# Two barriers of a layer replaced by waits for single producers, in a decoder step of retention, gated linear attention and RWKV-7

## The reference

```python
h = rmsnorm(x, norm_mix)
proj = h @ w_in                      # columns for retention, GLA, RWKV-7 and three merge gates
y_ret, S_ret = retention_branch(...) # 8 heads, key 64, value 128
y_gla, S_gla = gla_branch(...)       # 4 heads, key 128, value 256
y_rw, S_rw, shift = rwkv7_branch(...)# delta rule, 16 heads of 64
merged = (sigmoid(g0) * (y_ret @ wb[0]) + sigmoid(g1) * (y_gla @ wb[1])
          + sigmoid(g2) * (y_rw @ wb[2]))
x = x + merged @ w_out
h = rmsnorm(x, norm_ffn)
x = x + (swiglu(h) if layer == 0 else top2_of_8_experts(h))
```

## Time and profile before

| | us |
|---|---|
| median of 3 runs (2856.09 to 2858.42) | 2857.78 |
| the profiled execution, its own time | 2859.5 |
| span of that execution in the trace | 2857.3 |
| TensorE (PE) busy | 2717.4 (95%) |
| VectorE (DVE) busy | 841.7 (29%) |
| ScalarE (ACT) busy | 571.9 (20%) |
| mean granted TensorE clock | 0.979 of full |

### The profile page before, as it was taken

One profiled execution on the slowest core, in us unless ns is written; L12 is line 12 of the kernel. 1 busy time (PEld: TensorE's weight loads), 2 busy tenths in 40 slices (PEclk: granted clock), 3 DMA queues, 4 the chain that ended last, 5 costly groups with the idle time before them and its releaser, 6 DMA issues. The chain is left out here.

```text
span 2857.3 us, 78627 instructions
## 1 busy us (share of the span) xinstructions
PE 2717.4 (95%) x34890; PEld 2218.9 (78%) x34890; DVE 841.7 (29%) x2465; ACT 571.9 (20%) x1736; POOL 0.2 (0%) x4
## 2 busy tenths in 40 slices
PE   8999989999799999999998999989799999999998
PEld 5777877666577776777786676667799999999997
DVE  2023664555411001112465555531301111110111
ACT  2123332332200000113333323310110111111011
POOL 0000000000000000000000000000000000000000
PEclk9999999999999999999999999979799999999999
DMA  6333432222243444323343222224399999999985
GB/s 216 97 120 141 145 122 72 67 73 73 69 138 124 136 133 144 106 91 132 120 149 118 72 73 64 66 83 139 147 348 372 336 327 366 367 332 346 370 331 219
DMA packets 144460, 495.95 MB, mean 174 GB/s; under 512 B 18608, under 2 KB 23344, under 8 KB 141648
## 3 DMA queue, kind: packets, MB, share of 16 engines
q1 hardware_dynamic: 144208, 492.24, 48.6%
HBM read 471.88 MB, written 20.29 MB: 172 GB/s over the span
## 5 line engine op out<-in xcount | busy, mean ns | idle before, releaser
L378 PEld LDWEIGHTS psum<-work,ring 128*64 128x64 f32 x16896 | 699.9, 137 | 27.9 <-issue 14.5
L378 PE MATMUL psum<-work,ring 128*64 128x96 f32 x16896 | 714.9, 246 | 3.0 <-issue 1.7
L293 PE MATMUL psum<-hT,ring 128*128 128x288 f32 x2048 | 562.7, 416 | 0.0
L293 PEld LDWEIGHTS psum<-hT,ring 128*128 128x128 f32 x2048 | 375.6, 192 | 95.9 <-ACT work L389 2.7
L371 PE MATMUL psum<-hT,ring 128*128 128x288 f32 x1024 | 256.1, 411 | 7.8 <-PEq L188 7.8
L371 PEld LDWEIGHTS psum<-hT,ring 128*128 128x128 f32 x1024 | 196.8, 193 | 65.1 <-issue 10.2
L1400 ACT ACTIVATE work<-psum 128x256 f32<-128x256 f32 (+4 forms) x304 | 101.1, 370 | 426.3 <-PE psum L1314 100.1
L1803 PE MATMUL psum<-hT,ring 128*128 128x288 f32 x704 | 172.6, 409 | 1.7 <-DVE hT L1877 1.7
L1803 PEld LDWEIGHTS psum<-hT,ring 128*128 128x128 f32 x704 | 134.7, 191 | 39.6 <-issue 2.1
L2401 DVE TENSOR_TENSOR work<-psum,work 128x96 f32<-128x96 f32 x176 | 45.3, 257 | 380.8 <-PE psum L378 368.6
L2350 ACT ACTIVATE work<-psum 128x96 f32<-128x96 f32 x176 | 44.1, 250 | 410.0 <-PE psum L378 410.0
(11 more groups left out here) (399 smaller groups left out, 2892.9 us busy)
## 6 DMA issues: line engine op xcount, KB each, us to landing
ring<-w_ff_dram SPq DMA_DIRECT2D x540, 512.0 KB, 5.4
ring<-w_mix_dram SPq DMA_DIRECT2D x256, 512.0 KB, 3.7
ring<-w_ff_dram SPq DMA_DIRECT2D x72, 384.0 KB, 4.7
work<-s_gla_dram SPq DMA_DIRECT2D x8, 1024.0 KB, 4.8
gla_s_out<-work SPq DMA_DIRECT2D x8, 1024.0 KB, 4.6
work<-s_ret_dram SPq DMA_DIRECT2D x8, 512.0 KB, 4.7
ret_s_out<-work SPq DMA_DIRECT2D x8, 512.0 KB, 3.0
work<-s_rw_dram SPq DMA_DIRECT2D x16, 256.0 KB, 2.6
```

Of the source, the lines that this page charges most:

```text
L293: mm = nc.tensor.matmul(out, ring[:, s, k, :], rhs[:, k, :], start=(k == 0), stop=(k == KT - 1))
L378: mm = nc.tensor.matmul(out[64 * c:64 * c + 64], ring[:, s, k, 64 * c:64 * c + 64], rhs[:, k0 + k, :], start=(k0 + k == 0), stop=(k0 + k = ...
```

## The change

Each layer's projections and retention now share one block, and so do the delta rule and the merge. An engine runs from one program into the next with no barrier between. Two waits are added on TensorE: before retention for all 24 results of the projections to have left their banks, and in the second slab of the merge, before each of its eight products, for the tile of `y_rw` that it reads. The landing place of the 32-bit masks moves from column 8704 to 12000 of `work`. The semaphores of the two phases of a block are cleared together at the block's end.

```diff
-    masks32 = work[:, 8704:8704 + MASKS.shape[1]].bitcast(U32)
+    masks32 = work[:, 12000:12000 + MASKS.shape[1]].bitcast(U32)
...
-    def retention(nc, block, sig, layer):
+    def retention(nc, block, sig, layer, projected):
...
         @block.tensor
         def _(pe):
+            pe.wait_ge(projected("bank_free"), 3 * RING)
             with pe.Fori(0, PAIRS) as i:
...
-    def mix_out(nc, block, sig, layer):
+    def mix_out(nc, block, sig, layer, delta):
...
-                slab_products(pe, n % RING, bank[n % 4][:, 0:T], y_rw if n % 2 else [hT[:, k, :] for k in range(KT)])
+                x = y_rw if n % 2 else [hT[:, k, :] for k in range(KT)]
+                for k in range(KT):
+                    if n == 1:
+                        pe.wait_ge(delta("y"), k + 1)
+                    mm = nc.tensor.matmul(bank[n % 4][:, 0:T], ring[:, n % RING, k, :], x[k], start=(k == 0),
+                                          stop=(k == KT - 1))
+                mm.then_inc(slab_done, 1)
...
-        with phase(nc, f"in{layer}") as (block, sig):
-            project_in(nc, block, sig, layer)
-        with phase(nc, f"ret{layer}") as (block, sig):
-            retention(nc, block, sig, layer)
+        with phase(nc, f"in{layer}") as (block, projected):
+            project_in(nc, block, projected, layer)
+            retention(nc, block, Signals(nc, f"ret{layer}"), layer, projected)
         with phase(nc, f"gla{layer}") as (block, sig):
             gated_linear(nc, block, sig, layer)
-        with phase(nc, f"rw{layer}") as (block, sig):
-            rwkv(nc, block, sig, layer)
-        with phase(nc, f"mix{layer}") as (block, sig):
-            mix_out(nc, block, sig, layer)
+        with phase(nc, f"rw{layer}") as (block, delta):
+            rwkv(nc, block, delta, layer)
+            mix_out(nc, block, Signals(nc, f"mix{layer}"), layer, delta)
```

## The result

The changed kernel takes 2842.14 us, a median of 5 runs (2833.58 to 2846.41), against 2857.78 before (5 runs, 2856.09 to 2860.39). The ratio is 0.9942, with a 95% interval of 0.9923 to 0.9960: 11 to 22 us faster, 16.6 at the ratio itself. The ratio compares the means of the runs; the two medians lie 15.6 apart. Forecast were 2842.1 us and 0.9945.

A forecast was written before the change was run, and what follows sets the result against it. TensorE, busy 95% of the span, was taken as the bound, so time is won only where it idles or runs at the lower clock. 7.9 + 7.8 + 1.4 − 1.4 = 15.7 us off 2857.78 gave 2842.1, range 2835 to 2849.

The forecast's parts named there:

- Seam A: Projections to retention: without the barrier, 3.95 and 3.90 us gained in the two layers, together 7.9.
- the second wait: Before the first GLA slab: TensorE waits some 0.3 us for ScalarE's grant behind its table load.
- The drain behind a table load: Skill's rule, left out of the sum: grant before the first GLA slab 1.4 us later per layer, total gain 12.9.
- The clock at seam A: Projections to retention: 3.5 us of the 7.9 gained come from avoiding the lower clock.
- Seam B: Delta rule to merge: without the barrier, 7.8 us of idle time and 1.4 of clock gained.
- the clock's part of the gain: Merge's first slab: less time lost to the low clock, 1.4 us gained (0.6 to 2.2).
- The clears: End of each merged block: clearing two phases' semaphores together, with all engines waiting, loses 1.4 us.
- Only idle time is won: Rival: clock falls at projections to retention, returns no earlier at the merge; gain 10.8 us, 2847.0; chance 0.13.
- The barrier stays in another form: Rival: a block's two programs are still kept apart by something all engines pass; no change, 2857.8; chance 0.04.
- the code is not there: Rival: engines stall at the seams for the next program's instructions; slower, 2877.4 us; chance 0.03.
- The last step changes its clock: Rival: delta rule's last step, 6.0 us apart between layers, changes; 2848.1 or 2836.1 us; chance 0.12 each side.
- a later phase gives time back: Sign of being wrong: GLA and feed-forward should start earlier by the forecast sums and last as long as before.

The follow-up runs named there:

- filled barriers: Kernel before, barriers kept, with products nobody reads in TensorE's time in front of them at both seams; ratio 0.9990, 2.9 us faster.
- seam A alone: Changed kernel with delta rule and merge put back in separate blocks; ratio 0.9962 to the kernel before, 10.9 us faster.
- seam B alone: Changed kernel with projections and retention put back in separate blocks; ratio 0.9971 to the kernel before, 8.3 us faster.
- e4: Changed kernel, wait before retention cut to 22 of 24 results, VectorE granting the first GLA slabs; ratio 0.9941 to the kernel before.
- e5: e4 with the merge's first slab done in pieces within the delta rule's last step; ratio 0.9903 to the kernel before, median 2832.1 us.
- e6: e5 with seven of the eight products of the merge's second slab also moved into the last step; ratio 0.9910 to the kernel before.
- e7: Kernel before with 80 unused semaphores more in each of six phases; ratio 1.0016, 4.6 us slower.
- e8: e5 with three products of the merge's second slab done ahead of the variance; ratio 0.9885 to the kernel before, median 2827.8 us.
- e9: e5 with three products that nobody reads in the places where e8 moves products; ratio 0.9913 to the kernel before.

## Why the prediction was right

**Seam A** was put at 7.9 us and measured 7.8. Two things inside it were off and cancelled. TensorE starts its swaps 0.36 us after ScalarE's copy ends, where the sum had it start at once (0.44 behind the last slab): idle is 0.80, not 0.4 to 0.6. For that the second wait, for ScalarE's grant behind the table load, does not show at all, since the load (to 124.16) is over before the swaps are. The wait of some 0.3 us that the sum put there was not seen. The transposes start 5.74 us behind the last slab; 5.7 was forecast. The copies for the transposes did hide, and so did SP's load of the state. The drain behind a table load that the Trainium skill states ("ScalarE: Activation LUTs", What ACT_TABLE_LOAD costs) is not seen here either: the load starts at 1241.87 in layer 1 and ScalarE's next copy at 1243.16, 1.29 later, where the page's total would be 2.66.

**The clock at seam A**, 3.5 us of the 7.9, measured 3.4 (the ledger's 7.8 less 4.4 of idle). It is shown by the filled barriers: the same slab in 3.88 us with the barrier left in place.

**Seam B** was put at 9.2 and measured 9.0. The idle time went whole. The second slab starts 5.57 and 5.34 us behind the variance (4.9 to 5.7 forecast), the clock came back 4.3 and 4.1 us after the variance began (3.5 to 5.0). The slab lost 1.7 and 1.5 us to the low clock, at the upper end of the 1.05 to 1.85, so the clock's part of the gain was 1.2 where the sum had 1.4. The picture behind it was right for layer 1 only: the sum had the clock low from before the variance, and in layer 0 it was at 1.00 there and fell in the slab.

**The clears** were put at 1.4 and measured 1.5 in the ledger, of which 1.2 is the clears' own time. The kernel with the unused semaphores shows that such time is on TensorE's path.

**The rivals.** 'Only idle time is won' fell at A by the trace and by the seam's own interval. 'The barrier stays in another form' and 'the code is not there' fell with the first trace: TensorE is idle at no seam for more than 0.8 us, and not at all between the variance and the merge. 'The last step changes its clock' happened, in both directions in one trace. From the variance of the seventh pair of heads to that of the eighth, layer 0 and layer 1:

| kernel | layer 0, us | layer 1, us |
|---|---|---|
| before | 21.2 | 27.1 |
| after | 23.5 | 24.8 |
| seam A alone | 23.5 | 21.2 |
| seam B alone | 25.2 | 21.2 |
| barriers filled | 23.5 | 24.3 |
| e4 | 24.3 | 23.5 |
| e5 | 22.2 | 22.2 |
| e6 | 22.4 | 23.9 |
| e7 | 24.8 | 24.3 |
| e8, e9 | 21.7 | 21.7 |

These are single executions. Up to e4 and in e7 they lie anywhere between 21.2 and 27.1 with the same instructions, and the granted clock goes with them: 1.00 at 21.2, 0.85 at 23.5, 0.59 at 27.1. So the prediction's picture of two values 6.0 apart was too simple. In the ledger this step cost 2.3 in layer 0 and gave 2.3 in layer 1. In e5, e8 and e9 both layers agree and are near the shortest, with one product more in this stretch in e5 and four in e8 and e9. In e6, with eight more, they don't agree. One trace of each kernel can't show that the added work is what keeps the clock.

By its own sign, 'a later phase gives time back', the prediction would be wrong: two stretches of the ledger do, by 1.48 and 1.08. The first holds the 2.3 of this step, the second is the group of products above; in both TensorE runs the same instructions at another clock, and the same step gives 2.3 in the other layer. The sign could not tell such drift from a cost of the change. The forecast's own range of 2838 to 2846 isn't the sum of its named bounds either: added up they give 2840.1 to 2847.7. That the number came out within 0.1 us is luck of the median, since the changed kernel's runs lie 13 us apart (with mean clocks of 0.980 to 0.987), and the traced pair gave 18.2; that the terms came out within 0.3 us is not.

## What to carry to other kernels

Here a barrier cost TensorE idle time, a slower clock behind it, and the clear of its semaphores, and the three can be read apart: the bracket in the timeline, the first group behind it against a steady one, and the clear's own row. After a barrier is gone, look at what the freed engine could do instead of following on: here the merge's first slab, put into the gaps of the step before it, brought some 11 us by the ratios of e4 and e5, of which the traces give some 4.5 to the moved work. Move only as much as the last producer's delay allows: with three products of the second slab ahead of the variance the third slab starts 3.4 us behind it, not 5.6, and with seven the wait came back. And compare a step that changes its clock over several traces before a gain is put down to an edit.

## What the runs showed of the hardware that I had not expected

- A range clear's time grows with the semaphores in it: 196 ns for 29 names, 499 for 85, 567 for the 98 of the delta rule and the merge together, 629 for 109 (e7), some 5.4 ns a name.
- TensorE started 0.36 us after the end of ScalarE's last copy, for which it waits in front of retention's loop. Inside straight code it started 0.06 after its producer (in the changed kernel the square ends at 767.08 and the variance, which waits for it, starts at 767.14). In e4, where the wait is met early, the same loop starts with no idle time. What makes the difference of 0.3 no run shows.
- The kernel before took 2856.0, 2858.5 and 2860.5 us as the median of three groups of runs on three chips. Some microseconds between medians of different groups say nothing.
